# The attention masks are added on VectorE, by the instruction that finds the row maximum, instead of by a matmul with the identity

## What is computed

```
# "D" heads, 4 per hybrid layer: causal attention, q and k of width 96
logits = q @ k.T * scale ;  logits[key > query] = -inf ;  p = softmax(logits)
# "A" heads, 4 per hybrid layer: a causal top-128 choice of keys, with a bias by distance
score  = sum over index heads of relu(iq @ ik.T) * w ;  keep the top 128 keys of each query
logits = q @ k.T * scale + bias[bucket(query - key)] ;  others = -inf ;  p = softmax(logits)
# "E" heads, 8 in the even layer: three dilated branches merged, so each key counts
# as often as it is in a branch: p = softmax(q @ k.T + log(multiplicity)), -1e30 where it is 0
```

## Time and profile before

| | |
|---|---|
| time, median of 3 (lowest, highest) | 3794.53 us (3793.47, 3801.32) |
| span of the profiled execution | 3786.5 us |
| busy in it: TensorE, VectorE, ScalarE, GpSimd | 3551.4, 1744.2, 1125.4, 444.8 us |
| mean granted TensorE clock | 0.957 |

### The profile page before, as it was taken

The page is one execution under the profiler, slowest core; times in us unless marked ns, Lnnn a source line. Parts: engine busy times, 40 slices in busy tenths (PEclk is TensorE's granted clock), DMA queues, the critical chain, the costliest instruction groups (busy, mean ns, idle before and its releaser), DMA issues.

```text
span 3786.5 us, 39204 instructions
## 1 busy us (share of the span) xinstructions
PE 3551.4 (94%) x14372; PEld 2601.6 (69%) x14372; DVE 1744.2 (46%) x2378; ACT 1125.4 (30%) x1645; POOL 444.8 (12%) x263
## 2 busy tenths in 40 slices
PE   7999998999999999997999999976989999889998
PEld 5888673678887888763668886332668886568886
DVE  3332398533323332288543323897443326363322
ACT  3222334332223222334332222111232214432222
POOL 0000233100000000134100000476000001300000
PEclk9999997999999999998899999987999999989999
DMA  4333320023332333321023332100023332213332
GB/s 130 93 93 97 75 67 29 1 73 95 96 97 78 94 94 96 82 73 35 1 59 93 93 94 83 56 23 22 29 66 95 95 99 66 74 56 94 94 95 72
DMA packets 396814, 279.93 MB, mean 74 GB/s; under 512 B 35756, under 2 KB 373556, under 8 KB 396596
## 3 DMA queue, kind: packets, MB, share of 16 engines
q1 hardware_dynamic: 395896, 277.60, 24.9%
q10 hardware_dynamic: 828, 1.13, 0.1%
HBM read 276.59 MB, written 2.11 MB: 74 GB/s over the span
## 4 chain that ended last, share of the span: by engine, by line
PE 82%; DVE 12%; ACT 2%; issue 2%; DMA 1%; POOL 1%; SPq 0%; POOLq 0%; DVEq 0%; ACTq 0%
PE bank L723 23%; PE bank L722 23%; PE bank L721 23%; PE bank L716 1%; PE bank L984 1%; PE bank L965 1%; PE bank L966 1%; PE bank L1071 1%; DVE xn_lo L1654 1%; DVE arena L1753 1%; DVE xn L1644 1%; PE bank L973 1%; DVE arena L1732 1%; DVE small L1729 1%; PE bank L1128 1%
## 5 line engine op out<-in xcount | busy, mean ns | idle before, releaser
L723 PE MATMUL bank<-xn_lo,w_hi 128*128 128x512 f32 x2800 | 1116.9, 399 | 0.0
L721 PE MATMUL bank<-xn_hi,w_hi 128*128 128x512 f32 x2496 | 991.3, 397 | 54.8 <-DVE xn_lo L1654 51.3
L1659 DVE TENSOR_TENSOR w_lo<-wring,w_hi 128x1024 fp32r<-128x1024 f32 x434 | 536.8, 1238 | 1003.2 <-ACT w_hi L1269 986.2
L722 PE MATMUL bank<-xn_hi,w_lo 128*128 128x512 f32 x2496 | 990.0, 397 | 0.0
L1269 ACT ACTIVATE w_hi<-wring 128x1024 fp32r<-128x1024 f32 x490 | 514.5, 1052 | 569.0 <-DMA wring<-in_ffn_down 324.8
L723 PEld LDWEIGHTS bank<-xn_lo,w_hi 128*128 128x128 f32 x2800 | 530.0, 189 | 124.5
L721 PEld LDWEIGHTS bank<-xn_hi,w_hi 128*128 128x128 f32 x2496 | 472.8, 189 | 186.0 <-issue 54.3
L722 PEld LDWEIGHTS bank<-xn_hi,w_lo 128*128 128x128 f32 x2496 | 473.2, 190 | 110.6
L723 PE MATMUL bank<-h_lo,w_hi 128*128 (+1 forms) x1056 | 416.3, 394 | 0.0
L722 PE MATMUL bank<-h_hi,w_lo 128*128 (+1 forms) x1056 | 414.2, 392 | 0.0
L721 PE MATMUL bank<-h_hi,w_hi 128*128 (+1 forms) x1056 | 412.4, 391 | 0.0
(11 more groups left out here) (344 smaller groups left out, 3381.2 us busy)
## 6 DMA issues: line engine op xcount, KB each, us to landing
wring<-in_ffn_gate SPq DMA_DIRECT2D x88, 512.0 KB, 3.7
wring<-in_ffn_up SPq DMA_DIRECT2D x88, 512.0 KB, 3.7
wring<-in_ffn_down SPq DMA_DIRECT2D x88, 512.0 KB, 3.6
wring<-in_ffn_w_gate SPq DMA_DIRECT2D x44, 512.0 KB, 3.7
wring<-in_ffn_w_up SPq DMA_DIRECT2D x44, 512.0 KB, 3.7
wring<-in_ffn_w_down SPq DMA_DIRECT2D x44, 512.0 KB, 3.5
wring<-in_w_in SPq DMA_DIRECT2D x34, 512.0 KB, 3.6
wring<-in_w_out SPq DMA_DIRECT2D x16, 512.0 KB, 4.4
```

The lines of the kernel that those rows point to most:

```text
L721: nc.tensor.matmul(ps, w_hi[:, slot, t, 0:M], hi, start=start, stop=False)
L722: nc.tensor.matmul(ps, w_lo[:, slot, t, 0:M], hi, start=False, stop=False)
L723: return nc.tensor.matmul(ps, w_hi[:, slot, t, 0:M], lo, start=False, stop=stop)
L1659: nc.vector.tensor_tensor(w_lo[:, slot, :, :].rearrange("p k c -> p (k c)"), wunit[:, slot, :], w_hi[:, slot, :, :].rearrange("p k c -> p ...
```

## The change

For A and E units the product of the identity with the mask is gone from TensorE. In place of the reduction VectorE issues `tensor_tensor_reduce`, which reads the bank and the mask, writes the negative of their sum to the p buffer, and takes the minimum of it along the row, which is the negated maximum. ScalarE then takes exp of the p buffer in place, with scale -1. D units stay as they are. What waits for what changes with it: TensorE reuses the bank when the maximum is there (`att_max`) and not when exp is done; VectorE, not TensorE, waits for GpSimd's tile (`att_bm`); VectorE, not ScalarE, waits for the p buffer (`att_t`); and GpSimd's tile is free with `att_max`, not with `att_s`.

```
 pe_attention
-                        pe.e.wait_ge(att_exp.h, att_exp.by(pe.l, i - 3))
+                        taken = att_exp if units[i - 4][0] == "D" else att_max
+                        pe.e.wait_ge(taken.h, taken.by(pe.l, i - 3))
...
-                    nc.tensor.matmul(s[:, lo:N], q[:, tb * P:N], k[:, lo:N], start=True, stop=False)
-                    nc.tensor.matmul(s[:, lo:N], ident, msk, start=False, stop=True).then_inc(att_s.h, 1)
+                    if lo < N:
+                        nc.tensor.matmul(s[:, lo:N], q[:, tb * P:N], k[:, lo:N], start=True, stop=False)
+                        mm = nc.tensor.matmul(s[:, lo:N], ident, C("causal"), start=False, stop=True)
+                    mm.then_inc(att_s.h, 1)
 hyb_ready
-            if u in BM:
-                eng.e.wait_ge(att_bm.h, att_bm.by(eng.l, BM.index(u) + 1))
 act_attention
+                    else:
+                        nc.scalar.activation(p, p, ACT.Exp, scale=-1.0,
+                                             bias=nmax[:, c:c + 1], accum_out=psum_[:, c:c + 1]).then_inc(att_exp.h, 1)
 dve_attention
+                    if m == "D":
+                        nc.vector.tensor_reduce(nmax[:, c:c + 1], s, AX.X, ALU.max, negate=True).then_inc(att_max.h, 1)
+                    else:
+                        added = mask(dve, h, tb, i)
+                        if i >= 3:
+                            dve.e.wait_ge(att_t.h, att_t.by(dve.l, i - 2))
+                        nc.vector.tensor_tensor_reduce(p_buf(units, i)[:, 0:N], s, added, -1.0, -SENTINEL,
+                                                       ALU.add, ALU.min, nmax[:, c:c + 1]).then_inc(att_max.h, 1)
 pool_attention
-                    pool.e.wait_ge(att_s.h, att_s.by(pool.l, BM[n - 3] + 1))
+                    pool.e.wait_ge(att_max.h, att_max.by(pool.l, BM[n - 3] + 1))
```

More of the change, by code:

```diff
@@ L961, in pe_attention @@
                     q, k = ops["qk"](m, h)
-                    msk, lo = ops["mask"](m, h, tb, i)
+                    lo = tb * P if m == "D" else N
                     if lo:
-                        nc.tensor.matmul(s[:, 0:lo], q[:, tb * P:N], k[:, 0:lo], start=True, stop=True)
-                    nc.tensor.matmul(s[:, lo:N], q[:, tb * P:N], k[:, lo:N], start=True, stop=False)
-                    nc.tensor.matmul(s[:, lo:N], ident, msk, start=False, stop=True).then_inc(att_s.h, 1)
+                        mm = nc.tensor.matmul(s[:, 0:lo], q[:, tb * P:N], k[:, 0:lo], start=True, stop=True)
+                    if lo < N:
+                        nc.tensor.matmul(s[:, lo:N], q[:, tb * P:N], k[:, lo:N], start=True, stop=False)
+                        mm = nc.tensor.matmul(s[:, lo:N], ident, C("causal"), start=False, stop=True)
+                    mm.then_inc(att_s.h, 1)
                 if 2 <= i < U + 2:
@@ L992, in hyb_qk, with hyb_mask, even_mask @@
             return T(t_aq[h // 2])[r:r + 64, :], T(t_ak[h // 2])[r:r + 64, :]
-        def hyb_mask(m, h, tb, u):
-            if m == "D":
-                return C("causal"), tb * P
+        def hyb_mask(dve, h, tb, u):
             if tb == 0:
-                return bias[:, h, SEQ - P:SEQ], 0
-            return T(t_bm[BM.index(u) % 3])[:, 0:(tb + 1) * P], 0
+                dve.e.wait_ge(pro_sb.h, 4 + 2 + A_HEADS)
+                return bias[:, h, SEQ - P:SEQ]
+            dve.e.wait_ge(att_bm.h, att_bm.by(dve.l, BM.index(u) + 1))
+            return T(t_bm[BM.index(u) % 3])[:, 0:(tb + 1) * P]
+        def even_mask(dve, h, tb, u):
+            return C("lnmult")[:, SEQ - (tb + 1) * P:]
         def hyb_v(m, h, b):
@@ L1016, in hyb_ready @@
                 eng.e.wait_ge(mn_x.h, mn_x.by(eng.l, 4))
-                eng.e.wait_ge(pro_sb.h, 4 + 2 + A_HEADS)
-            if u in BM:
-                eng.e.wait_ge(att_bm.h, att_bm.by(eng.l, BM.index(u) + 1))
-        HYB = dict(qk=hyb_qk, mask=hyb_mask, v=hyb_v, ready=hyb_ready)
+        HYB = dict(qk=hyb_qk, v=hyb_v, ready=hyb_ready)
         def att_free(pe, m):
@@ L1042, in even_ready @@
                 eng.e.wait_ge(ez_sb.h, len(E_Z))
-        EVEN = dict(qk=even_qk, mask=lambda m, h, tb, u: (C("lnmult")[:, SEQ - (tb + 1) * P:], 0),
+        EVEN = dict(qk=even_qk,
                     v=lambda m, h, b: e_vv[:, b, h * E_DIM:(h + 1) * E_DIM], ready=even_ready)
@@ L1413, in act_attention @@
                     act.e.wait_ge(att_max.h, att_max.by(act.l, i + 1))
-                    if i >= 3:
-                        act.e.wait_ge(att_t.h, att_t.by(act.l, i - 2))
                     c = i % 4
-                    nc.scalar.activation(p_buf(units, i)[:, 0:N], pb[(0, 1, 4, 5)[i % 4]][:, 0:N], ACT.Exp,
-                                         bias=nmax[:, c:c + 1], accum_out=psum_[:, c:c + 1]).then_inc(att_exp.h, 1)
+                    p = p_buf(units, i)[:, 0:N]
+                    if units[i][0] == "D":
+                        if i >= 3:
+                            act.e.wait_ge(att_t.h, att_t.by(act.l, i - 2))
+                        nc.scalar.activation(p, pb[(0, 1, 4, 5)[i % 4]][:, 0:N], ACT.Exp,
+                                             bias=nmax[:, c:c + 1], accum_out=psum_[:, c:c + 1]).then_inc(att_exp.h, 1)
+                    else:
+                        nc.scalar.activation(p, p, ACT.Exp, scale=-1.0,
+                                             bias=nmax[:, c:c + 1], accum_out=psum_[:, c:c + 1]).then_inc(att_exp.h, 1)
                 u = i - 4
@@ L1836, in dve_mixers, with dve_attention @@
                                                in1=T(t_or[pr]), op0=ALU.mult, op1=ALU.mult).then_inc(o_n.h, 1)
-        def dve_attention(dve, units, st, order):
+        def dve_attention(dve, units, st, order, mask):
             U = len(units)
@@ L1845, in dve_attention @@
                     dve.e.wait_ge(att_s.h, att_s.by(dve.l, i + 1))
[L1846 to L1847 removed]
+                    s = pb[(0, 1, 4, 5)[i % 4]][:, 0:N]
+                    m, h, tb = units[i]
+                    if m == "D":
+                        nc.vector.tensor_reduce(nmax[:, c:c + 1], s, AX.X, ALU.max, negate=True).then_inc(att_max.h, 1)
+                    else:
+                        added = mask(dve, h, tb, i)
+                        if i >= 3:
+                            dve.e.wait_ge(att_t.h, att_t.by(dve.l, i - 2))
+                        nc.vector.tensor_tensor_reduce(p_buf(units, i)[:, 0:N], s, added, -1.0, -SENTINEL,
+                                                       ALU.add, ALU.min, nmax[:, c:c + 1]).then_inc(att_max.h, 1)
                 if 1 <= i < U + 1:
@@ L2225, in _ @@
                 dve_mixers(dve)
-                dve_attention(dve, HYB_UNITS, STAGES["out", l], Y_HYB)
+                dve_attention(dve, HYB_UNITS, STAGES["out", l], Y_HYB, hyb_mask)
                 dve_take(dve, STAGES["out", l], add)
@@ L2235, in _ @@
             dve_even(dve)
-            dve_attention(dve, E_UNITS, STAGES["out", "even"], Y_EVEN)
+            dve_attention(dve, E_UNITS, STAGES["out", "even"], Y_EVEN, even_mask)
             dve_take(dve, STAGES["out", "even"], to_r)
```

## The result

The changed kernel takes 3848.2 us (median of four runs, 3838.8 to 3853.6) where the kernel before, on the same chip, takes 3794.0: a ratio of 1.0133, with a 95% interval of 1.0116 to 1.0151. It is 54 us slower, where 24 us less were forecast. The executions compared in this document are all in the chip's faster state; one of the kernel that computes the scores twice, at 3888.0 us, was not and is left out. The profiled execution has a span of 3851.4 us and took 3853.2.

A forecast was written before the change was run, and what follows sets the result against it. TensorE was taken to bound plain E groups, VectorE the group with weight splits. Gains of 13.9 us (even layer) and 10.4 (two A layers), 24.3 in all, took 3794.5 to 3770 us; range 3760 to 3785.

The forecast's parts named there:

- The bound: E groups: TensorE bounds a plain group of 9.85 us; VectorE is full in the group with four weight splits.
- What goes, and the change of form that stays: Mask steps on TensorE, 2.64 us a group, go; 0.19 us lost changing form 64*128 to 128*128 stays, before the transposes.
- Rival 3: Behind the scores: the form change costs nothing, so 0.19 us a unit also goes; 36 us gained, 3758; chance 0.08.
- The pair, x = 0.10: VectorE's two new instructions cost x = 0.10 us more than the 0.69 us reduction at 512 keys.
- Rivals 1 and 2: VectorE's pair: 1, scan rate, 3782, 0.18 including between cases; 2, fixed cost makes VectorE the bound, 3810, 0.05.
- The plain E group, 7.61 us: E group without splits falls from 9.85 to 7.61 us, including a 0.40 us wait before the 384-key transposes.
- E's sum, 13.9 us: Even layer's eight E groups: gain of 13.9 us in all, five plain groups giving 11.2.
- The A groups: Hybrid layers: GpSimd, released by the maximum, delays the scaling at 512 keys; gain 5.2 us a layer, 10.4 for two.
- The 8.53 of the others: A groups after the first take 8.53 us, TensorE waiting 1.32, where they took 10.90 and 10.16.
- Rival 4: E groups: the clock falls to 1.2 GHz, a group takes 13.0 us, the kernel 3844, +50; chance 0.03.
- The sum of 24.3 us: Whole kernel: 13.9 us from the even layer plus 10.4 from two A layers gained, giving 3770.

The follow-up runs named there:

- the kernel with the start filled: Changed kernel plus an identity product into the score bank ahead of the scores, in the first A head and first E head only: 3824.7 us, 1.0066.
- the last kernel: Changed kernel with weight splits spread, GpSimd's sum later, identity product in the first E head and in 512-key A units before the scaling wait: 3769.3 us, 0.9930.

## Why the prediction was wrong, step by step

- **The bound (TensorE in a plain E group, VectorE in the group with splits): right.** Every experiment at full clock bears it out.
- **What goes, and the change of form that stays: right.** Behind the 512-key scores the transposes start 1.05 us after them (2670.79 to 2671.84), as the mask did (2643.57 to 2644.62). Rival 3, that the 0.19 us go too, is false here; and the rule of the Trainium skill, "TensorEngine Tiling (Array Packing)", Key Properties, that a change of tiling mode drains the engine, agrees with this trace. Scores of the D units, of form 96\*128, go over to the mask product of form 128\*128 without the gap: in the trace of the kernel before, 128 columns of each start 0.22 us apart (700.22 and 700.44), where behind the form 64\*128 it is 0.41 (711.78 and 712.19).
- **The pair, x = 0.10: right, a little high.** The main instruction takes 692 ns, the second 82 ns beside the reciprocal's start; the reciprocal starts 0.62 us behind the start of the pair (2671.95 to 2672.57 in the kernel with the start filled), where it started 0.60 behind the reduction in the earlier trace rows, so x is about 0.02. Rivals 1 and 2 fall. What the Trainium skill, "DVE: opcode table, instruction layouts, handler registers and perf-mode slots", Datapath and trigger behaviour, says of a stage that reads its own last result agrees: no trace of the scan's 1.22.
- **The plain E group, 7.61 us: right at a clock of 1.00** (7.63), with one wait, in front of the transposes of 384 keys: 0.18 us shown idle, 0.40 expected from the scores' streaming.
- **E's sum, 13.9 us: nearly right at that clock.** The stretch takes 61.0 us in the last kernel, where it took 73.3: 12.3 less, its filler in the first head included; up to the first weight product behind it, 67.1 against 80.3 us, 13.3 less. With the splits spread the full group is gone, which the sum did not have.
- **The A groups: the mechanism right, the term untested.** GpSimd starts with the reciprocal behind the pair and holds the 384-key scaling for 1.45 us (1.3 expected). The first group is 10.07 (10.6 by the sum, "about 10" in the text). The 8.53 of the others, with GpSimd in the way and the clock at 1.00, never ran. In the last kernel, with a split in each group, they take 8.41, 8.92 and 8.91, and from the first A scores to the first weight product behind attention either layer takes 40.3 us where it took 45.7: 5.4 less, where 5.2 were expected. That the totals agree is luck in part: the parts forecast were -0.4, 2.37, 1.63 and 1.63, and the first three groups gained 1.75, 1.98 and 1.25.
- **Rival 4, the fallen clock: this was the step that failed**, not by its price but by its chance. It said 13.0 us for a group and 3844 for the kernel; the E groups take 13.4 and the kernel 3848. (The nearness of the totals is partly luck: the A groups, priced like E's, take 10.07, 15.43 and 13.85.) It got 0.03, on the ground that TensorE "stays busy some 70%, with waits of at most 1.3 us". Two things were wrong there. The waits were worked out for groups without other work in VectorE's queue, but the clock falls at the exceptions, and the same prediction names all of them: the pile of weight splits, GpSimd before the scaling, GpSimd's old work at E's start. Where the first two meet, a split of 1.22, the pair of 0.69 and a scaling held by GpSimd stand one behind the other on VectorE; their wait was never added up, and the trace has 2.28 us. And even 1.3 was no safe bound: the longest wait in the attention of the kernel before was 0.95 us, and pauses of 1.21 and 1.25 us stand right ahead of the fall in two of the experiments, and shortly ahead of it in a third. The earlier trace rows had one stretch of low clock, with half of the time idle, and one without any pause. It had nothing between, and a share of 70% lay between. That was an unknown with two bounds, and only one of them was taken into the range.
- **The sum of 24.3 us: near the gain of a kernel whose clock holds.** The last experiment is such a kernel, and gains 27 us (19 to 34 by its interval); its three stretches, up to the weight products, gain 24.0. It is not the kernel that was forecast, though: the splits are spread, GpSimd starts later and fillers are added, so the sum for the plain change at full clock was never measured.

## What to carry to other kernels

Before work is taken off TensorE, look at each place where it will wait afterwards, the worst ones first (other work in VectorE's queue, GpSimd beside a scaling, the first unit of a stage), and price the whole stretch at half clock as well; if no stretch of the trace with such pauses kept its clock, the low clock deserves a real chance. When many matmuls take twice as long at a "busy" TensorE, read the granted clock before anything else. A pause can be shortened by moving what is queued on the other engine, or filled by a product nobody needs, placed in the wait and into a bank that is overwritten: here 1.1 us of such work in each of a few units made the difference between 3789 and 3769.

## What the runs showed of the hardware

- In the A and E stretches the granted clock went from 1.00 to 0.50 behind single pauses of 1.2 to 2.3 us between short matmuls, and the matmuls behind took about twice as long (512-key scores 2.07 us in place of 1.12). In the changed kernel that lasted until the weight products behind attention, at E some 100 us. With products of the masks' size in every group the clock came back after 7 to 20 us. Waits of up to 0.95 us, within the attention of the kernel before, had no fall behind them.
- It is no fixed function of the instructions. One kernel held 1.00 through two pauses of 1.21 us in layer 0 and fell at the third, and in layer 1 fell at the first. At E's start, with all mask products in place and no pause of attention ahead, the kernel before held in its profiled execution, and two others fell there (the one with the splits spread, and the one with the A masks alone on VectorE). What tips it was not found.
- An instruction that adds two operands of 128x512 float32 (one from PSUM), writes the result and keeps its minimum takes 692 ns on VectorE, as long as a plain reduction (691). The instruction that writes its result per row is shown with 82 ns, and the next one starts at the same time.
- VectorE's scaling of 384 columns, SBUF to SBUF, takes 0.42 us alone. Beside GpSimd's addition it ended 0.2 us behind that (0.73 us in the earlier trace rows, 1.45 in the changed kernel). Moving GpSimd's start by one instruction brought the mean from 678 to 421 ns.
